# Ten modulation chunks inside the scan mixer instead of batches of four around it

## The reference, cut to what matters

```python
s = jax.nn.silu(c)
for l in range(2):
    mod = s @ ada_w[l] + ada_b[l]
    sh1, sc1, g1, sh2, sc2, g2 = [m[:, None, :] for m in jnp.split(mod, 6, axis=-1)]
    h = rmsnorm_2(x, norm1_w[l]) * (1.0 + sc1) + sh1
    mix = hybrid_mixer(h, w_in[l], ...)
    x = x + g1 * mix
    h = rmsnorm_2(x, norm2_w[l]) * (1.0 + sc2) + sh2
    ff = swiglu_2(...) if l == 0 else moe_swiglu(...)
    x = x + g2 * ff
```

## Time and profile before

| | |
|---|---|
| median of 3 runs | 3024.08 us |
| the profiled execution's own time | 3024.89 us |
| its span | 3023.1 us |
| PE busy | 2746.3 us (91%) |
| DVE busy | 1903.1 us (63%) |
| ACT busy | 1323.3 us (44%) |
| granted clock of TensorE, mean | 0.944 |

### The profile page before, as it was taken

One profiled execution on the slowest core, in us unless ns is written; L12 is line 12 of the kernel. 1 busy time (PEld: TensorE's weight loads), 2 busy tenths in 40 slices (PEclk: granted clock), 3 DMA queues, 4 the chain that ended last, 5 costly groups with the idle time before them and its releaser, 6 DMA issues. The chain is left out here.

```text
span 3023.1 us, 58145 instructions
## 1 busy us (share of the span) xinstructions
PE 2746.3 (91%) x22862; PEld 1953.9 (65%) x22862; DVE 1903.1 (63%) x2920; ACT 1323.3 (44%) x1601; POOL 10.0 (0%) x12
## 2 busy tenths in 40 slices
PE   6988899898987889988899988789999999999997
PEld 3544577676544457756667756657777777777775
DVE  2165455555125646524456525469999999999998
ACT  1044144343011534402144303137777777777774
POOL 0000000000100000000000000000000000000000
PEclk9988999999997899998899998889999999999999
DMA  6250355455356045543465543229999999999994
GB/s 280 81 212 1 139 207 203 156 206 195 118 236 248 1 160 208 191 189 146 157 226 196 193 185 126 105 92 372 353 367 354 355 368 354 365 354 353 367 356 189
DMA packets 124086, 677.23 MB, mean 224 GB/s; under 512 B 13808, under 2 KB 14288, under 8 KB 69200
## 3 DMA queue, kind: packets, MB, share of 16 engines
q1 hardware_dynamic: 122256, 664.80, 59.0%
q10 hardware_dynamic: 1728, 11.01, 1.0%
HBM read 674.71 MB, written 1.05 MB: 224 GB/s over the span
## 5 line engine op out<-in xcount | busy, mean ns | idle before, releaser
L771 PE MATMUL ps<-projected,normed_or_mix 128*128 (+2 forms) x5088 | 1034.5, 236 | 47.7 <-DVE normed_or_mix L756 22.7
L772 PE MATMUL ps<-projected,normed_or_mix 128*128 (+2 forms) x5088 | 1032.4, 236 | 0.0
L771 PEld LDWEIGHTS ps<-projected,normed_or_mix 128*128 128x128 bf16 x5088 | 499.6, 98 | 175.1 <-DVE normed_or_mix L756 67.1
L925 ACT ACTIVATE normed_or_mix<-weights 128x2048 bf16<-128x2048 f32 x304 | 578.6, 1903 | 0.0
L772 PEld LDWEIGHTS ps<-projected,normed_or_mix 128*128 128x128 bf16 x5088 | 500.1, 98 | 33.9
L773 PE MATMUL ps<-projected,normed_or_mix 128*128 (+2 forms) x2544 | 519.3, 237 | 0.0
L773 PE MATMUL ps<-projected,aux 128*128 (+2 forms) x2544 | 512.3, 235 | 0.0
L756 DVE TENSOR_TENSOR normed_or_mix<-weights,normed_or_mix 128x2048 bf16<-128x2048 f32 x159 | 364.0, 2289 | 56.2 <-ACT normed_or_mix L925 47.9
L756 DVE TENSOR_TENSOR aux<-weights,normed_or_mix 128x2048 bf16<-128x2048 f32 x159 | 363.5, 2286 | 22.4 <-ACT normed_or_mix L925 21.8
L623 PE MATMUL ps<-weights,turned 128*128 128x384 f32 (+2 forms) x960 | 300.2, 476 | 12.9 <-PEq L471 7.6
L794 ACT ACTIVATE probs<-ps 128x128 f32<-128x128 f32 (+1 forms) x318 | 97.6, 307 | 453.3 <-PE ps L773 452.5
(11 more groups left out here) (336 smaller groups left out, 3314.1 us busy)
## 6 DMA issues: line engine op xcount, KB each, us to landing
weights<-moe SPq DMA_DIRECT2D x224, 1024.0 KB, 7.0
weights<-moe SPq DMA_DIRECT2D x224, 512.0 KB, 7.1
weights<-l_ffn SPq DMA_DIRECT2D x66, 1024.0 KB, 5.1
weights<-ada SPq DMA_DIRECT2D x64, 1024.0 KB, 5.8
weights<-l_ffn SPq DMA_DIRECT2D x66, 512.0 KB, 5.5
weights<-ada SPq DMA_DIRECT2D x64, 512.0 KB, 6.1
weights<-ffn SPq DMA_DIRECT2D x28, 1024.0 KB, 5.0
weights<-w_in SPq DMA_DIRECT2D x16, 1024.0 KB, 6.1
```

What stands on the lines that cost most here:

```text
L771: pe.matmul(o, hi, h_hi(k), start=(k == 0), stop=False)
L772: pe.matmul(o, hi, h_lo(k), start=False, stop=False)
L925: act.activation(gu[parity(j)][0], RING[:, s, 0:2 * D], ACT.Copy).then_inc(S.hi_gu.sem, 1)
```

## The change

The ring's plan has all the chunks of a layer in one run of ten between w_in and w_out. `modulate` takes no chunks in these two layers. The mixer takes ten. All of them use bank 7 of PSUM, so that the rows of chunk i wait for the column copy of chunk i-1 (`ada_out`). On PE, chunk 0 stays where chunks 0 and 1 were, chunks 1 to 4 stand between the products of the mixer, and chunks 5 to 9 come behind L1676, each chunk's rows followed by its turn. On ACT the copies of chunks 5 to 7 stand ahead of the squares that the norm needs, and those of 8 and 9 behind them. The decays per chunk are 16 products with one column instead of 8 with two, and stand ahead of the state space sums; the table `dec` is indexed accordingly.

```diff
@@ -260,12 +260,9 @@
...
     for layer in range(2):
-        planned("ada", 4, 44 + 12 * layer)
         planned(f"w_in{layer}", len(chunks(L2N)) + 2)
-        planned("ada", 4, 48 + 12 * layer)
+        planned("ada", 10, 44 + 10 * layer)
         planned(f"w_out{layer}", len(chunks(D)))
-        if layer == 0:
-            planned("ada", 4, 52)
         planned("ffn2" if layer == 0 else "moe", F2 // PB * (1 if layer == 0 else NE))
...
-    ada_bank = lambda i: PS[:, (7, 6, 7, 0)[i], :]
+    one_bank = PS[:, 7, :]
 
     def ada_row(pe, i):
         arrived(pe, place.n + i)
+        if i >= 1:
+            pe.wait_ge(S.ada_out.sem, S.ada_out.at(i))
         for turn_ in range(KD // strips):
             for j in range(strips):
                 k = turn_ * strips + j
-                mm = pe.matmul(ada_bank(i)[32 * j:32 * (j + 1), 0:WC], CS[:, k, :],
+                mm = pe.matmul(one_bank[32 * j:32 * (j + 1), 0:WC], CS[:, k, :],
                                RING[:, (place.n + i) % SLOTS, k * WC:(k + 1) * WC],
                                start=(turn_ == 0), stop=(turn_ == KD // strips - 1))
         mm.then_inc(S.ada_rows.sem, 1)
...
         act.wait_ge(S.ada_rows.sem, S.ada_rows.at(i + 1))
-        if i >= 2:
-            act.wait_ge(S.ada_cols.sem, S.ada_cols.at(i - 1))
         release(act)
-        act.activation(adar[:, i % 2, :], ada_bank(i)[:, 0:WC], ACT.Copy).then_inc(S.ada_kept.sem, 1)
+        act.activation(adar[:, i % 2, :], one_bank[:, 0:WC], ACT.Copy).then_inc(S.ada_kept.sem, 1)
...
@@ -1554,9 +1551,7 @@
                     mm = pe.matmul(PS[:, 1, b * T:(b + 1) * T], alT[:, b * PB:(b + 1) * PB], aw, start=True, stop=True)
                 mm.then_inc(M.la_product.sem, 1)
                 ada_row(pe, 0)
-                ada_row(pe, 1)
                 ada_turn(pe, 0)
-                ada_turn(pe, 1)
...
                 mm.then_inc(M.cums.sem, 1)
+                for c in range(4):
+                    o = c % 2 * 64
+                    for h in range(4):
+                        mm = pe.matmul(PS[0:64, 0, 256 + c * 4 + h:257 + c * 4 + h], la[:, c // 2, h * 64:(h + 1) * 64],
+                                       blkg[:, o:o + 1], start=True, stop=True)
+                mm.then_inc(M.decays.sem, 1)
 
...
                 mm.then_inc(M.cum_made.sem, 1)
-                for h in range(4):
-                    for b in range(2):
-                        mm = pe.matmul(PS[0:64, 0, 256 + 4 * h + 2 * b:258 + 4 * h + 2 * b], la[:, b, h * 64:(h + 1) * 64],
-                                       blkg[:, 0:PB:64], start=True, stop=True)
-                mm.then_inc(M.decays.sem, 1)
                 pe.wait_ge(M.xb_made.sem, M.xb_made.at(6))
-                pe.wait_ge(S.ada_out.sem, S.ada_out.at(2))
...
                     mm.then_inc(M.seg_made.sem, 1)
+                ada_row(pe, 1)
 
                 pe.wait_ge(M.xh_kept.sem, M.xh_kept.at(3))
                 for u in range(8):
@@ -1620,6 +1616,7 @@
                                    start=True, stop=True)
                     if u % 4 == 3:
                         mm.then_inc(M.scored.sem, 1)
+                ada_turn(pe, 1)
...
                 mm.then_inc(M.ss_made.sem, 1)
+                ada_row(pe, 2)
...
                                            st[:, h, c - 1, :], start=False, stop=True, skip_group_check=True)
                     mm.then_inc(M.out_made.sem, 1)
+                    ada_turn(pe, 2 + b)
+                    ada_row(pe, 3 + b)
 
...
                     mm = pe.matmul(PS[:, 6 - 5 * g, 0:T], XB[r, 5, PB:2 * PB], SS[r, :], start=True, stop=True)
                 mm.then_inc(M.off_made.sem, 1)
-                for i in range(2, batch):
+                ada_turn(pe, 4)
+                for i in range(5, batch):
                     ada_row(pe, i)
-                for i in range(2, batch):
                     ada_turn(pe, i)
 
...
                         ins = dve.scalar_tensor_tensor(
-                            out=st[:, h, c, :], in0=st[:, h, c - 1, :], scalar=dec[:, 4 * h + c:4 * h + c + 1],
+                            out=st[:, h, c, :], in0=st[:, h, c - 1, :], scalar=dec[:, c * 4 + h:c * 4 + h + 1],
...
                 ada_row_kept(act, 0)
-                ada_row_kept(act, 1)
...
                     if c == 3:
                         ada_cols_kept(act, 0)
-                        ada_cols_kept(act, 1)
...
                     act.activation(seg[:, u, :, :], seg[:, u, :, :], ACT.Exp).then_inc(M.seg_exp.sem, 1)
+                ada_row_kept(act, 1)
+                ada_cols_kept(act, 1)
+                ada_row_kept(act, 2)
                 for b in range(2):
                     act.wait_ge(M.out_made.sem, M.out_made.at(b + 1))
                     act.activation(sc4[b], PS[:, 2 + b, :], ACT.Square).then_inc(M.out_squared.sem, 1)
-                for i in range(2, batch):
+                    ada_cols_kept(act, 2 + b)
+                    ada_row_kept(act, 3 + b)
+                ada_cols_kept(act, 4)
+                for i in range(5, batch - 2):
                     ada_row_kept(act, i)
+                    ada_cols_kept(act, i)
                 act.wait_ge(M.y_gated.sem, M.y_gated.at(1))
                 for b in range(2):
                     ins = act.activation(off, y[:, b, :], ACT.Square, accum_out=y_ss[:, b:b + 1])
                     if b == 0:
                         act_step(act, ins)
                 ins.then_inc(M.y_squared.sem, 1)
-                for i in range(2, batch):
+                for i in range(batch - 2, batch):
+                    ada_row_kept(act, i)
                     ada_cols_kept(act, i)
         M.done()
         ada_done(batch)
 
     for layer in range(2):
...
         lay = 2 + layer
-        modulate([(X, lay, 0, 2)], col("n_mix", lay * KD, KD), rows=2 + layer, batch=4,
-                 loads=((aw, d["gla_a_w"][layer]),))
+        modulate([(X, lay, 0, 2)], col("n_mix", lay * KD, KD), rows=2 + layer, loads=((aw, d["gla_a_w"][layer]),))
...
         linear(ht, KD, L2N, lambda c0: range(2), store2, cols_major=CONV)
-        scan_mixer(layer, 4)
+        scan_mixer(layer, 10)
         projected_by(2, [(gate_row, lay, 2, 2)], add_gated(X))
         checkpoint(nc, f"s{layer}_mix", X)
-        modulate([(X, lay, 3, 2)], col("n_ffn", lay * KD, KD), batch=4 * (1 - layer),
-                 gates=[(gate_row, lay, 5, 2)])
+        modulate([(X, lay, 3, 2)], col("n_ffn", lay * KD, KD), gates=[(gate_row, lay, 5, 2)])
```

More of the change, by code:

```diff
@@ L1519, in ada_turn @@
         for m in range(per):
-            t = pe.matmul(ada_bank(i)[:, WC + 4 * m:WC + 4 * m + 3], adar[:, i % 2, m * PB:(m + 1) * PB], fold[:, 0:3],
+            t = pe.matmul(one_bank[:, WC + 4 * m:WC + 4 * m + 3], adar[:, i % 2, m * PB:(m + 1) * PB], fold[:, 0:3],
                           start=True, stop=True)
@@ L1534, in ada_cols_kept @@
         act.activation(ada[:, c * per:(c + 1) * per, :],
-                       ada_bank(i)[:, WC:WC + 4 * per].rearrange("p (m c) -> p m c", c=4)[:, :, 0:3],
+                       one_bank[:, WC:WC + 4 * per].rearrange("p (m c) -> p m c", c=4)[:, :, 0:3],
                        ACT.Copy).then_inc(S.ada_out.sem, 1)
```

## The result

| | before | after |
|---|---|---|
| median | 3024.26 us (7 runs) | 3053.0 us (7 runs) |
| lowest and highest | 3019.72, 3029.56 | 3040.72, 3057.53 |
| the profiled execution | 3024.89, span 3023.1 | 3058.49, span 3056.6 |
| granted clock of TensorE, mean | 0.944 | 0.937 |

The ratio of the mean times is 1.0082, 95% interval 1.0059 to 1.0104: slower by 0.8% (the medians lie 28.7 us apart, 0.95%). The runs after fall in two groups, 3041 to 3042 us (three) and 3053 to 3057.5 us (four); the profile is of one like the upper group.

The account below looks back on a forecast made before the run. Mixers were taken as bound by DVE's convolution, then mostly PE at low clock. Per mixer 2.3 + 2.3 + 4 + 14 = 22.6, twice 45.2, less 11.2 for modulate and about one: 3058 us; 8-in-10 range 3033 to 3077.

Parts of the forecast that it names:

- Modulate: Three modulate calls without their four chunks each come down to 10.59 us: 3.7 us each, together 11.2 us gained.
- First third: Mixer start: more decay products ahead of the small sums, perhaps at low clock; 0 to 3.2 us, taken as 2.3.
- the slow end: Start of the mixer: clock stays low behind one lone chunk, so PE's sums end 3.2 us later.
- the chunk of rows 9: Chunk in the profile before, said to stand alone and run slow in rows and turn; evidence for low clock.
- Chunks 1 and 2: Ahead of the chunk states: chunk 1 costs rows and turn, chunk 2 fits a gap; 2.3 us fast, 4.9 slow; took 2.3.
- L1655 to L1676: Output stretch with chunks 3 and 4: rows and turns half slow, part of the clock's gain; -3.7 to +9.4, taken +4.
- the first rival: Clock stays up from chunk 1 to the mixer's end: 12.8 us per mixer, 3039 us; chance 0.18.
- Behind L1676: Mixer's end: five serial chunks over one bank, 3.5 us each fast, 5.4 slow; +9.2 to +19.3, taken +14 per mixer.
- the fast bound: Behind L1676 with all chunks at the fast pace: 19.3 us against 10.13 before, so 9.2 us more.
- Behind the mixers: After the mixer PE may come out with its clock up, speeding slow L455: about one us taken off.
- the second: Rival: clock stays down, 34.2 us per mixer, less 11.2 for modulate: +57, 3082 us; chance 0.14.
- The rival of no loss: Clock up all the way and into the next block: 5.9 us per mixer, +0.6 in all, 3025 us; chance 0.07.

Follow-up runs that it names:

- The decay products alone: Kernel before, with only 16 one-column decay products put ahead of the four small sums: 3023.97 us, ratio 0.9995.
- the run with 0 and 1 in front: Changed kernel, but chunks 0 and 1 together in front in two banks, as before; chunks 2 to 9 as changed: 3032.65 us, ratio 1.0020.
- the run with two banks: Changed kernel, but chunks behind L1676 alternate between banks 0 and 7, next chunk's rows sent ahead of the last one's turn: 3039.68 us, ratio 1.0046.
- earlier squares: Changed kernel, but ACT squares the gated output behind the copies of chunk 5, not chunk 7: 3050.21 us, ratio 1.0079.
- the run with modulate bare: Kernel before, without the twelve chunks of its three modulate calls, their columns zero, mixers keeping their four: 3014.98 us, ratio 0.9965.

## Why the prediction was right, and where its steps were off

*Modulate.* As predicted. From the first DVE work to the end of L553 it is 10.60 us in layer 0, in both calls:

```profile
1303.58 1.23 DVE L535 TENSOR_TENSOR normed_or_mix<-x_sb 128x1024 f32<-128x1024 f32 x1 [0.30 <-PEq L931]
...
1310.47 3.71 DVE L553 TENSOR_SCALAR turned<-ps,mod_scale,modulations 128x256 f32<-128x256 f32 x8 [1.10 <-PE ps L521]
```

No wait for row parameters came, and PE waited for no w_out load behind either mixer. The call in layer 1 came down to the same length from 14.85 us, not from the 14.3 assumed, so the calls gave 11.7 us and not 11.2. Alone this part is worth 10.1 us by the run.

*First third.* +2.3 predicted, +1.96 and +2.10 measured, and by the mechanism named: behind one chunk the clock stayed low, L1558 took 2.07 us where its like took 1.13, and the decay products 3.57 us. DVE waited for the small sums:

```profile
1414.00 0.17 DVE L1722 COPY small<-ps 128x16 f32<-128x16 f32 x1 [3.89 <-PE ps L1572]
```

The decay products alone, at the clock of before, cost nothing, so the term is the clock's. But two chunks in front don't secure the clock: in the run with 0 and 1 in front, layer 1 has the 21.1 us all the same. The reason given for the slow end was weak: the chunk of rows 9 did not stand alone, the turn of another ended 0.36 us ahead of it.

*Chunks 1 and 2.* This step failed in its size: +2.3 was taken, the fast price, since "the clock is up before L1618". It was up, rows of chunk 1 took 1.50 and its turn 0.83, but it fell behind the turn, and L1631 then took 5.11 us where 3.10 us stand in the trace of the run with 0 and 1 in front and in that of before:

```profile
1426.93 3.10 PE L1634 MATMUL ps<-projected,aux 64*64 64x128 f32 x24
```

The rows of chunk 2, behind it, took 2.79 us and no longer fitted into the gap. +4.9 was the upper bound, and +4.86 and +4.63 came, for chunk 1 by another way than that bound assumed. I had charged the chunk at its own price and not for what it does to the clock of the work behind it.

*L1655 to L1676.* +4 predicted, +4.61 and +4.90 measured. Rows and turns at mixed clock, as assumed: with their waits 8.0 us in layer 0 (rows 2.79, turns 0.83 and 1.04), where the term has 7.4. The clock gave back 3.4 us, in the short products alone (L1655 0.49 instead of 0.80); L1670 was still at 7.09 us. The run with 0 and 1 in front shows what was possible: 0.4 us more than before in layer 0, and 0.7 less in layer 1. That is the first rival's condition for the middle, met by another place of chunk 1. That the clock can rise there without it is seen once, in layer 1 of the run with two banks.

*Behind L1676.* This step failed in its size too: +14 was too large, +10.26 and +10.35 came. The mechanism is shown (two banks take 5.5 and 6.7 us from it, earlier squares nothing), and so is the pace of 3.45 us, the 3.5 of the prediction. I had put half of the chunks at the slow pace; only chunk 4's turn and chunk 5's rows were slow, and from 1465 on the clock was up. The +9.2 of the fast bound was nearly the value.

*Behind the mixers.* -1 for a faster L455: its like L452 took 2.02 us instead of 3.75, and the block behind the mixer of layer 0 2.51 us less, but 0.29 more in layer 1. Not in the sum were -1.7 us in the w_in products of layer 1 (L620 takes 55.97 us where L623 took 57.66) and +4.3 behind the start of the last modulate. Of these, 1.6 us stand in one group of small products (L1914 is L1910 of before):

```profile
1951.15 5.35 PE L1910 MATMUL ps<-column_params,turned 128*128 128x8 f32 x32 [1.33 <-PEq L471]
```

```profile
1980.36 6.96 PE L1914 MATMUL ps<-column_params,turned 128*128 128x8 f32 x32 [1.15 <-PEq L468]
```

Windows over 40 us from the start of that modulate show the lower clock, of after and of before:

```profile
1969.00:2009.00 40.00, 22.98 (x111) 21.15 (x112) 20.94 (x79) 7.30 (x11) 0.00 (x0) 0.62 0.12 50
```

```profile
1940.00:1980.00 40.00, 23.02 (x115) 20.30 (x116) 22.41 (x82) 7.30 (x11) 0.00 (x0) 0.70 0.12 50
```

The other 2.6 us lie behind the start of the expert stages, and what brings them is not shown. The new mixers are not needed for it: the run with modulate bare, whose mixers have the old instructions, takes 3.5 us more than before from the same mark to the end.

The forecast, +33 us, met the +33.6 of the profiled execution in part by luck, because errors cancelled: per mixer one term was 3.7 us too large and another 2.5 too small, which left the two mixers 1.5 us under the forecast, and outside of them 10.1 us were gained instead of 12.2. The median, 3053.0 us, is 5 us under the forecast; the profiled execution was slower than all seven runs of the median.

*The rivals.* The clock did not stay up, nor down: the windows of the mixers give 0.70 and 0.72. The 3082 of the second took the fast price, 2.3 us, for chunks 1 and 2; by the slow price of 4.9 it should have been 3087. The first rival's 3039 is near the lower group of runs, 3041 us, with a mean clock of 0.942 to 0.944 against 0.936 to 0.941; but no trace of that group was caught, so which stretch of it ran faster stays open. The mixer of layer 1 in the run with two banks shows one stretch that can: the output, 3.8 us shorter with its instructions unchanged. The rival of no loss was not met by the change, but by its cures: the ten chunks fit when two of them stand in front and the last have two banks.

What the change cost in the mixers is thus shown in two parts. One is the single bank behind L1676, 12 us of the two mixers. The other is chunk 1 moved from the front into the middle, 13 us in each mixer: 4.7 and 5.5 at its own place, 4.2 and 5.6 in the output stretch, 1.9 behind L1676, and in layer 0 2.1 in the front. With both undone the mixers take 68.1 us, 4.2 more than before, which is what the six further chunks cost there. That the second part works through the clock is read from the windows and durations; what in chunk 1's place makes the clock fall was not separated further.

## What to carry to other kernels

Where a stage changes between the two levels of the clock, an inserted piece is to be charged with what the work behind it does at the lower level, and its place is worth trying: here the same six chunks made a mixer of 65 to 66 us or of 62 to 64. Filling a tail is free only as far as the tail's own chain covers it, and only with enough buffers that the filler's steps overlap: with one PSUM bank a chunk took 3.45 us here, with two 2.6. A good idea can be lost in its placement; ten chunks in the mixer made 1.0082 and, with two edits, 0.998.

## What the runs showed that I had not expected

- Row products (32 x 384, four side by side) that were put among short products cost no time in the stretch that holds them, if chunk 1 stood in front. With the rows and turns of two chunks in it the output stretch took 17.5 to 18.9 us in the eight mixers of four kernels (granted clock 0.82 in the slower, 0.90 in the faster). With none it took 17.5 to 19.0 us in the ten mixers of five kernels, among them the kernel before (18.4 and 18.3 us at 0.52 and 0.53).
- PE was busy for all of 19.00 us at clock 0.50, and busy for 19.30 of 29.00 us at 1.00, in one kernel: in these windows the granted clock follows neither the busy share nor the idle time. The Trainium skill ("TensorE: Matmul & The Clock Gate", Part 1) has activity release the throttle; by these two windows being busy is not enough, and the serial run's waits of 0.36 and 0.76 us did not take the clock away.
- The same front with two chunks took 19.0 us in layer 0 and 21.1 in layer 1 in four kernels alike, and 19.2 and 19.0 in the kernel before. What sets the two layers apart is not shown. Times of stages far from any edit also shifted by 2 to 4 us between kernels.
